# The down-projection of a PEER layer on one core: half of the third token tile's output channels gathered per expert instead of multiplied

## The reference, cut to what matters

```
act = gelu(einsum('btd,btrkd->btrk', h, u_table[experts]))   # up
w   = gates * act
y   = einsum('btrk,btrkd->btd', w, v_table[experts])         # down: 128 rows of 2048 per token
h   = layer_norm(alpha * h + y + ple, ln2_g, ln2_b)
```

## Time and profile before

| | |
|---|---|
| median of the runs | 4075.22 us |
| the profiled execution, its own time | 4074.44 us |
| its span in the trace | 4072.7 us |
| TensorE clock granted, whole span | 0.994 |
| PE busy | 3985.2 us (98%) |
| DVE busy | 2757.2 us (68%) |
| POOL busy | 1946.7 us (48%) |
| ACT busy | 1354.4 us (33%) |
| down-projection | 2991 to 4047 us, then the end of the layer norm and the stores to 4072.7 |

### The profile page before, as it was taken

One profiled execution on the slowest core, in us unless ns is written; L12 is line 12 of the kernel. 1 busy time (PEld: TensorE's weight loads), 2 busy tenths in 40 slices (PEclk: granted clock), 3 DMA queues, 4 the chain that ended last, 5 costly groups with the idle time before them and its releaser, 6 DMA issues.

```text
span 4072.7 us, 60798 instructions
## 1 busy us (share of the span) xinstructions
PE 3985.2 (98%) x21953; PEld 3460.1 (85%) x21953; DVE 2757.2 (68%) x3610; ACT 1354.4 (33%) x1637; POOL 1946.7 (48%) x1034
## 2 busy tenths in 40 slices
PE   6999999999999999999999999999999999999997
PEld 5888888878786888889999999999878888888886
DVE  7555555556504569987777777777358777878778
ACT  3333333342214222334444444444223333332322
POOL 7344444434442444457877887882033423333331
PEclk9999999999999999999999999999999999999998
DMA  5444444433432237677888888863657787787875
GB/s 217 152 152 152 152 152 152 152 124 139 175 140 83 93 114 258 232 258 218 234 234 238 235 236 235 236 172 108 237 217 308 296 321 300 297 322 296 318 289 196
DMA packets 343218, 859.19 MB, mean 211 GB/s; under 512 B 98488, under 2 KB 180424, under 8 KB 276968
## 3 DMA queue, kind: packets, MB, share of 16 engines
q1 hardware_dynamic: 163656, 559.52, 38.4%
q10 hardware_dynamic: 101664, 164.19, 11.6%
q0 software_dynamic: 77824, 134.52, 11.2%
HBM read 771.35 MB, written 222.03 MB: 244 GB/s over the span
## 4 chain that ended last, share of the span: by engine, by line
PE 52%; issue 30%; POOL 13%; DVE 1%; DMA 1%; DVEq 0%; POOLq 0%; ACT 0%; ACTq 0%; SPq 0%
POOL wlo L717 13%; PE bank L1624 8%; PE bank L1625 8%; PE bank L1626 8%; PE bank L1566 8%; PE bank L1568 8%; PE bank L1567 8%; PE bank L1285 1%; PE bank L1287 1%; PE bank L1286 1%; DMA raw<-in_weights 1%; DVE res L1639 0%; DVE stat L1643 0%; DVE xt L1683 0%; DMA h_lo<-h_d 0%
## 5 line engine op out<-in xcount | busy, mean ns | idle before, releaser
L717 POOL TENSOR_TENSOR wlo<-raw,whi 128x1024 fp32r<-128x1024 f32 x296 | 768.0, 2615 | 1011.6 <-ACT whi L885 462.8
L779 POOL DMA_INDIRECT gates_d<-sel_g,place_u x384 | 752.4, 1959 | 188.5 <-issue 95.2
L1285 PE MATMUL bank<-h_hi,whi 128*128 128x512 f32 x1712 | 674.3, 394 | 1.0 <-DMA h_lo<-h_d 0.5
L1287 PE MATMUL bank<-h_hi,wlo 128*128 128x512 f32 x1712 | 666.9, 390 | 0.0
L1286 PE MATMUL bank<-h_lo,whi 128*128 128x512 f32 x1712 | 666.3, 389 | 0.0
L1624 PE MATMUL bank<-whi,ew_hi 128*128 128x512 f32 x1536 | 598.5, 390 | 9.0 <-DVE wlo L1639 9.0
L1625 PE MATMUL bank<-wlo,ew_hi 128*128 128x512 f32 x1536 | 598.2, 389 | 0.0
L1626 PE MATMUL bank<-whi,ew_lo 128*128 128x512 f32 x1536 | 598.2, 389 | 0.0
L794 POOL DMA_INDIRECT row<-v_rows_d,expert_u x128 | 213.2, 1666 | 630.0 <-DVE res L2247 531.2
L1566 PE MATMUL bank<-h_hi,p_hi 128*128 128x256 f32 x1600 | 453.7, 284 | 2.8 <-DVE p_lo L1639 2.1
L1567 PE MATMUL bank<-h_lo,p_hi 128*128 128x256 f32 x1600 | 453.5, 283 | 0.0
(11 more groups left out here) (318 smaller groups left out, 7592.8 us busy)
## 6 DMA issues: line engine op xcount, KB each, us to landing
raw<-in_weights SPq DMA_DIRECT2D x338, 1024.0 KB, 5.0
v_rows_d<-in_weights ACTq DMA_DIRECT2D x96, 1024.0 KB, 7.7
x_raw<-in_weights SPq DMA_DIRECT2D x50, 1024.0 KB, 5.2
v_rows_d<-in_weights SPq DMA_DIRECT2D x32, 1024.0 KB, 6.9
gates_d<-zeros SPq DMA_DIRECT2D x32, 768.0 KB, 10.1
act_d<-mt ACTq DMA_DIRECT2D x128, 192.0 KB
act_in<-act_d SPq DMA_DIRECT2D x32, 768.0 KB, 7.8
gate_in<-gates_d SPq DMA_DIRECT2D x32, 768.0 KB, 10.2
```

The lines of the kernel that those rows point to most:

```text
L717: pool.tensor_tensor(wlo[slot][:, part], raw[slot][:, part], whi[slot][:, part].bitcast(F32), ALU.subtract).then_inc(lo_made, 1)
L779: pool.indirect_dma_start(out=places_d, out_offset=bass.IndirectOffsetOnAxis(ap=place_u[:, t, k:k + 1], axis=0), in_=sel_g[:, t, k:k + 1], ...
L1285: pe.matmul(bank[:, :], whi[slot][:, cols], rhs_hi[:, c, :], start=c == 0, stop=False)
L1287: last = pe.matmul(bank[:, :], wlo[slot][:, cols], rhs_hi[:, c, :], start=False, stop=c == DC - 1)
```

## The change

- **Third tile, half sparse.** For tile 2 (`T_PART`) channels 1024 to 2047 (c = 2, 3) are no longer multiplied. For each of its 128 picks POOL gathers a half row of 4 KB per token (`gather_part`) and DVE adds it (`add_part`, 1024 channels). Slabs of c = 0, 1 keep three tiles (36 matmuls), slabs of c = 2, 3 have two (24): 240 matmuls a pair in place of 288.
- **Word gathers doubled.** A pick now needs two activations (tile 3 and tile 2); `gather_act(k)` issues both, and after the first eight picks they are issued one pick at a time, between the gathers of the rows: per pick POOL issues row, half row, word, word.
- **Rings.** Rows and half rows have three buffers each (`ROWS` = 3); the row gather waits for `row_used` and the half row gather for `part_used`, three picks back.
- **Kept banks.** For c = 2, 3 and tiles 0, 1 the sums stay in four PSUM banks over all 16 pairs and are added to `res` once, in the last pair: six evacuations a pair in place of 12. The slabs come in the order c = 0, 2, 0, 2, 1, 3, 1, 3.
- **`ew` in four pieces** of 768 columns in place of eight of 384.
- **DVE's order.** Each slab's step begins with `add_row()`, which waits for its row, before `low_part`; it ends with `add_part()`. In 12 of the pairs a ninth row or half row is added, so that the last pair has two picks left. The end of the layer norm is rearranged (mean and gain in one instruction, standard deviation and bias in another, ACT only takes the root). Before the stage DVE makes the addresses of the half rows and their words, some 15 small instructions.

```diff
+T_PART, C_PART, PARTS = TD - 1, 2, 2
+V_SLABS = ((0, 0), (2, 0), (0, 1), (2, 1), (1, 0), (3, 0), (1, 1), (3, 1))
+KEPT = ((2, 0), (2, 1), (3, 0), (3, 1))
+V_EVACS = ((0, 0), (0, 1), (0, 2), (1, 0), (1, 1), (1, 2))
+ROW_EXTRA, PART_EXTRA = (1, 3, 5, 7, 9, 11), (2, 4, 6, 8, 10, 12)
-ROWS = 4
+ROWS = 3
...
+            def gather_act(k):
+                for to, of, cell in ((act_p, cells_d, cell_u), (act_c, cells_cd, cell_cu)):
+                    pool.indirect_dma_start(out=to[:, k:k + 1], out_offset=None, in_=of,
+                                            in_offset=bass.IndirectOffsetOnAxis(ap=cell[:, k:k + 1], axis=0)
                                             ).then_inc(act_landed, 16)
...
+            def gather_part(k):
+                pool.indirect_dma_start(out=part_row[k % ROWS][:, :], out_offset=None, in_=parts_d,
+                                        in_offset=bass.IndirectOffsetOnAxis(ap=part_u[:, k:k + 1], axis=0)
+                                        ).then_inc(part_landed[k % ROWS], 16)
...
-            gather_acts(0)
-            for k in range(1, PICKS):
-                if k % 8 == 0:
-                    pool.wait_ge(act_landed, 16 * k)
-                    gather_acts(k // 8)
+            for k in range(8):
+                gather_act(k)
+            for k in range(PICKS):
                 if k >= ROWS:
                     pool.wait_ge(row_used, k - ROWS + 1)
-                gather_row(k)
+                if k > 0:
+                    gather_row(k)
+                if k >= ROWS:
+                    pool.wait_ge(part_used, k - ROWS + 1)
+                gather_part(k)
+                if k + 8 < PICKS:
+                    if k % 8 == 0:
+                        pool.wait_ge(act_landed, 32 * (k + 8))
+                    gather_act(k + 8)
...
+            def add_row():
+                k = len(rows_added)
+                if k == PICKS:
+                    return
+                batch_weights(k)
+                dve.drain()
+                dve.wait_ge(row_landed[k % ROWS], 16 * (k // ROWS + 1))
+                dve.scalar_tensor_tensor(res[:, TD, :], row[k % ROWS][:, :], act_p[:, k:k + 1], res[:, TD, :],
                                          ALU.mult, ALU.add).then_inc(row_used, 1)
+                rows_added.append(k)
+
+            def add_part():
...
+                dve.wait_ge(part_landed[k % ROWS], 16 * (k // ROWS + 1))
+                at = res[:, T_PART, 512 * C_PART:]
+                dve.scalar_tensor_tensor(at, part_row[k % ROWS][:, :], act_c[:, k:k + 1], at, ALU.mult, ALU.add
+                                         ).then_inc(part_used, 1)
...
+            for J in range(PAIRS - 1):
+                nxt = (J + 1) % 2
+                add_row()
+                low_part(J, 1)
+                if J > 0:
+                    evacuate(J - 1, 1, 2, 6, 3)
+                make_weights(J, nxt, 0)
+                add_part()
+
+                add_row()
+                low_part(J, 2)
+                add_part()
+
+                add_row()
+                low_part(J, 3)
+                evacuate(J, 0, 0, 2, 1)
+                evacuate(J, 0, 1, 2, 2)
+                split_weights(J, nxt, 0)
+                add_part()
...
+                if J in ROW_EXTRA:
+                    add_row()
+                if J in PART_EXTRA:
+                    add_part()
+                dve.drain()
```

More of the change, by code:

```diff
@@ L371, in build_trunk @@
     row_landed = [sm(f"row_landed{i}") for i in range(ROWS)]
+    part_used = sm("part_used")
+    part_landed = [sm(f"part_landed{i}") for i in range(ROWS)]
     dve_lo_made = sm("dve_lo_made")
@@ L1604, in _, with expert_pair, slab @@
             pe.wait_ge(outs_added, 7 * FAST + 14)
[L1606 to L1614, removed]
-                        if t == 0:
-                            pe.wait_ge(dve_lo_made, U_LATE + 8 * J + 2 * c + k + 1)
-                        if k == 0:
-                            pe.wait_ge(v_added, TD * (4 * J + c) + t + 1)
+            def expert_pair(J, now, first=False, last=False):
+                def slab(m, tiles):
+                    c, k = V_SLABS[m]
+                    for t in tiles:
+                        bank = ps[V_BANK[c, t]]
+                        if t == 0:
+                            pe.wait_ge(dve_lo_made, U_LATE + 8 * J + m + 1)
+                        if k == 0 and (c, t) in EVAC_WAITS:
+                            pe.wait_ge(v_added, V_EACH * J + EVAC_WAITS[c, t])
+                        begins = k == 0 and ((c, t) not in KEPT or first)
+                        ends = k == 1 and ((c, t) not in KEPT or last)
                         hi, lo = ew_hi[now][k], ew_lo[now][k]
@@ new lines, in _ @@
+            add_row()
+            low_part(J, 1)
+            evacuate(J - 1, 1, 2, 6, 3)
+            add_row()
+            low_part(J, 2)
+            for n in range(PICKS - len(rows_added)):
+                add_row()
+            for n in range(PICKS - len(parts_added)):
+                add_part()
+            low_part(J, 3)
+            evacuate(J, 0, 0, 2, 1)
+            evacuate(J, 0, 1, 2, 2)
+            dve.drain()
+            for c in range(4):
+                quarter(res, TD, c)
@@ new lines, in _ @@
+            dve.drain()
+            variance(TD)
+            low_part(J, 4)
+            evacuate(J, 0, 2, 2, 3)
+            dve.wait_ge(ln2_landed, 32)
+            centre(TD)
+            stats(0)
+            low_part(J, 5)
+            evacuate(J, 2, 0, 3, 1)
+            evacuate(J, 2, 1, 3, 2)
+            finish(TD, 0)
+            low_part(J, 6)
+            stats(2)
+            quarter(res, T_PART, 3)
+            low_part(J, 7)
+            for t in range(T_PART):
+                evacuate(J, 1, t, 6, t + 1)
```

274 lines of the change are left out of this document (156 added, 118 removed).

## The result

The changed kernel takes 4175.98 us, the median of four runs (4172.58 to 4181.07), beside 4076.28 us of the kernel before: a ratio of 1.0246 (95% interval 1.0228 to 1.0263). The forecast was 4131 with a range of 4020 to 4210. Sign and range held; the loss is 100 us where 56 were forecast. The profiled execution's span is 4173.4 us.

The account below looks back on a forecast made before the run. DVE and POOL, level at 60.9 us a pair, plus POOL's 5.6 us descriptor wait give 32.5 us per four picks; 3018 start, 975 for 30 cycles, then the last pairs and end: span 4129, about 4131 us, range 4020 to 4210.

Parts of the forecast that it names:

- picks 0 to 119, first to last: Stage of the picks that carry words: 30 cycles of four picks at 32.5 us each, 975 us.
- PE gains only if it stays the bound, and it does not: Matmuls: 240 a pair take 54.4 us, 10.9 less, 174 us over 16 pairs; but DVE needs more, so PE waits.
- DVE per pair: DVE's adds, subtracts, evacuations and weights: 59.0 us a pair, 60.9 in pairs 1 to 12 with a ninth row or half row.
- DMA per pair: DMA engines: 24.9 MB a pair, 60.7 us by bytes at 410 GB/s or 63.6 us by shares.
- rival B: DMA engines bound at 63 to 65.2 us a pair: 4075 us, range 4045 to 4095; chance 0.14.
- POOL per pair: POOL's issue of 34 gathers a pair in place of 16, at 1.79 us each: 60.9 us.
- The late issue: POOL waits for descriptor space about every 16 gathers (four picks), until earlier gathers land: 5.6 us, bounds 3.3 and 8.9.
- Start: Before the first row add: 16 word gathers issued by 3018; PE waits until about 3024, some 24 us.
- End: After PE's last matmul: evacuation, statistics, three 2.3 us instructions with backlog, 17.5, and the store 4.4: 22 us.
- A: POOL never waits for descriptor space; DVE and POOL at 60.9 us a pair bound: 4027 us, range 4000 to 4050; chance 0.33.
- C: PE's clock: one two-tile slab in eight at 1.2 GHz adds 5 us a pair to the forecast: 4206 us; chance 0.08.
- D: The change does not do what it says, DVE stays behind words and nothing moves: 4075 us; chance 0.02.

Follow-up runs that it names:

- The two kernels whose share was 0.97 and 0.99: Changed kernel, early evacuation in both: with room for 120 descriptors and fewer tile 2 word gathers, 4091.68 us; with the row add narrowed to 512 columns, 4082.72 us.
- the edit: Changed kernel with the evacuation of (c = 1, tile 2) moved to the last step of its own pair: 4161.35 us.

## Why the prediction was right in sign and short in size

The forecast had DVE and POOL level and let POOL's wait for descriptor space decide. The runs show that POOL's own gathers decide: they are longer in the changed kernel than in the one before, the wait for space is shorter than forecast, and a wait for a PSUM bank that the sum did not have comes on top.

**The sum by its own steps**, on the profiled execution (4129 forecast, 4173.4 measured):

| step | forecast | measured | difference |
|---|---|---|---|
| POOL has issued the first 16 words | 3018 | 3023.08 | +5 |
| picks 0 to 119, first to last | 975 | 1005.8 | +31 |
| from there to the last pair on PE | 61 | 60.9 | 0 |
| PE's last pair | 53 | 64.4 | +11 |
| after PE's last matmul | 22 | 19.1 | -3 |

(3023.08 is the start of the first half row gather, 4028.91 that of the 121st; PE began the last pair at 4089.78 and ended it at 4154.2. The first word gather went out at 2999.74, 4.4 later than before.)

**PE gains only if it stays the bound, and it does not**: right. PE is busy 82%.

**DVE per pair**, 60.9: right within 2 us. DVE was busy for 59.0 where it was fullest (the run with the 2 KB gathers and 26 gathers a pair), and for 59.4 in the changed kernel (768.24 / 925 x 71.5).

**DMA per pair**, 24.9 MB and 60.7 to 63.6 us: the bytes are right (350 GB/s x 71.5 = 25.0 MB), the time was short. 0.93 x 71.5 is 66.5 us; 0.99 x 65.0 is 64.4. The two kernels whose share was 0.97 and 0.99 took 66.1 and 65.0 us a pair and 4092 and 4083 in all, near rival B's 63 to 65.2 and 4075 and within its range. B named the next bound; it did not decide here.

**POOL per pair**, 60.9: this step failed, by its smallest number. 1.79 us a gather "with DVE as busy as it is now" was taken into a kernel in which a gather meets DVE more often: 364 of 442 began in a DVE instruction with two SBUF inputs (82%), in the kernel before 125 of 228 (55%). (711.25 + 442 x 0.30) / 442 is 1.91, and with all waits by issue 2.0. Times 34 that is 68 us, over DVE, the DMA engines, PE and the old pair. Even without the late issues it is 65 us: over DVE's 59, and level with the DMA engines. The upper bound for the half row gather, 2.1 with its gap, was exceeded as well: 2.39.

**The late issue**, 5.6 us for 16 gathers: existence and frequency right, size wrong. 26 late issues of over 0.5 us in 442 gathers are one in 17; beyond the usual gap they last 1.5 us each (39 us), and up to 1.7 more since the gather then meets DVE's add (2.67 in place of 0.95): 3.2 in all, just under the lower of the two bounds. With 3.2 in place of 5.6 the forecast's own sum gives 30.9 us for four picks and 926 for the 120, 80 less than measured. DVE's waits for rows came as often as forecast, 27 in 925 us, but with 2.7 us on the average. The landing that is waited for was wrong too: not that of all gathers issued before, nor of a row one or two gathers back, but of the row five gathers back, while the row issued last needs another 3.1 to 7.8 us. That is why so few are late: from a row gather to the half row gather five places on it takes 10.4 us in the median, and a row lands after 8.5 (5.4 to 11.2). Why it is that landing stays open.

**What the forecast missed** made up for it. The four kept banks were costed as fewer evacuations and nothing else. That they leave four banks for the six other sums of a pair, so that a pair's first slab waits for an evacuation queued behind a row add and a `low_part`, stood in the diff (the bank numbers) and had no line in the sum. PE waited 138 us for it and DVE 64 us for the roundings that came late; the edit was worth 15 us by itself, of which some 5 in the stage, and 27 beside the larger descriptor space (4163.69 to 4136.72). So the measured 8.41 us a pick and the forecast's 8.12 are near each other partly by luck: a wait taken at nearly twice its price, against two terms too small or absent.

**Start**: PE stood still for 25.27 us, to 3029.36, forecast 24 and 3024. **End**: the fused end was worth 3 more than summed, and the wait for ACT's root in the last pair, which cost PE 8.49, was overlooked: of a moved step each wait counts, with what is queued ahead of its releaser.

**The rivals.** A (no wait for descriptor space, 4027) is false by the first batch of the run with 120 places. Its limit was miscalculated: the forecast's cycle is 30.7 us at a wait of 3.0, not 2.5. C (PE's clock) is there in small: a granted clock of 0.91 in the stage. 157 of the 3114 matmuls start some 0.43 us after the one before, 31 us more in all than at 0.2267, or 2.4 us a pair where C put 5. PE also waits 164 us in the stage, so it could make up a part of this; no run shows how much of it the time contains. D is false.

## What to carry to other kernels

Work that is moved from a full engine to gathers is paid three times: as issue time on POOL, as bytes, and as adds on DVE, and a gather that begins in a DVE instruction with two SBUF inputs takes what is left of that instruction and some 0.8 us more; so multiply the number of gathers by a duration of the kernel after, not of the kernel before. Reckon all resources to the same unit (here a pair): POOL 68, DMA 66, DVE 59 and PE 54 against 65.3 say that removing the first bound buys little more than what lies above the second. And where buffers or banks are dedicated to one use, look up who waits for those that are left.

## What the runs showed of the hardware that was not expected

- A gather over 128 partitions takes nine places of each of POOL's descriptor queues: seven fit in 64, thirteen in 120; the next one came 1.96 to 2.06 us late even with DVE idle.
- A gather's time on POOL is 0.95 us if DVE stands still or runs an evacuation at its start (78 of the 442 in the stage) and 1.76 on the average if DVE runs an instruction with two SBUF inputs (364), a subtract (`tensor_tensor`) as well as an add of a row. Its number of bytes hardly matters (half row gathers of 2.02 us with 2 KB, 2.09 with 4; undisturbed, a word and a row both 0.95).
- In the changed kernel, where the descriptor space is short, a late half row gather waits for one certain landing, that of the row gather five before it, and goes out 0.52 us after it.
- The DMA engines kept a share of 0.99 over 925 us. They moved 382 GB/s in it, 386 for a full share; the kernel before, with 16 gathers a pair and not 34, moves 304 / 0.79 = 385 for a full share in the same stretch. So the 415 of a stretch of 20 us was too high to reckon a whole pair with: 24.9 MB at 385 are 64.7 us, where the forecast had 60.7 by bytes.
